# Windowed attention with two masked key blocks: merging the halves by a predicated copy, the sink as a score column, and a reordered unit loop

## The chip, the cores and the metric

The kernel runs on one core of one Trainium2 chip. The metric is the device time of one launch in microseconds. Engines are named as in the profile: PE is TensorE (matrix products and transposes), DVE is VectorE, ACT is ScalarE, POOL is GpSimd, SP is the queue that starts the DMAs.

## The reference, cut to what matters

Two layers of a decoder are computed for a prompt of 2048 tokens and for eight short sample sequences. The second layer's token mixer is sliding-window attention with 16 query heads, four key heads, head size 64, a bias that falls with distance, and one learned sink per head. For the prompt, 128 queries see the 128 keys of their own block and the 128 of the block before:

```python
qi = jnp.arange(BLOCK)[:, None]
si = jnp.arange(2 * BLOCK)[None, :]
dist = BLOCK + qi - si
valid = (dist >= 0) & (dist < WINDOW) & ((blk - 1) * BLOCK + si >= 0)
s = einsum(q, k) * HEAD_DIM ** -0.5 - slopes * dist
s = jnp.where(valid, s, NEG_INF)
p = softmax(concatenate([s, sink_col], axis=-1))[..., :-1]
o = einsum(p, v)
```

With BLOCK = WINDOW = 128, key j of the block before is valid for query i where j > i, and key j of the query's own block where j <= i. So of every pair of columns (j, 128 + j) exactly one is valid, except in the very first block, which has no block before it.

## The kernel before, in words

The tokens are worked through in five chunks of 4, 3, 3, 3 and 3 blocks of 128 prompt tokens; chunks 1 to 4 also carry two sample sequences of four tokens each. For each chunk the kernel runs a fixed list of projections (`ORDER`): the recurrent layer (X, G, O, Z, P), then the attention layer's keys, values, queries (k, v, q), its gate projections (g), and after the attention the output projections (o, z, p). A projection of one 128-wide output block is 24 matmuls (eight steps over the input features, three products each, since fp32 operands are split into a high and a low part). Every engine runs a program written out by hand in this order, and semaphores tie the engines together. DMAs have their own queue, SP, which only loads weights, tokens and states.

The change is in the attention stage, `attention(g)`, of which each engine has its own copy. It works in units: one unit is one block of 128 queries (`b`) and four heads (`quad`), so chunk 0 has 16 units and every other chunk 12. For a unit

- PE computes the scores of four heads against 256 keys (`unit_scores`, L1269, 12 matmuls into PSUM banks 4 and 5),
- DVE adds the distance bias and the mask (L1011, four operations of 256 columns; a masked place has the distance 1e33), takes the row maximum (L1000), compares it with the sink (L1001), negates it (L1002) and prepares the sink's exponent (L1003),
- ACT takes the exponentials with their row sums (L750, four operations) and that of the sink (L752),
- DVE adds the sink to the sums (L1024), inverts them (L1025) and multiplies the rows by the result (`divide`, L1027, four operations of 256 columns, each with a column of scalars),
- PE turns the probabilities (`unit_turn`, L1282, eight transposes of 128 by 128 into banks 6 and 7), ACT copies them to SBUF (L777), PE multiplies them by the values (`unit_values`, L1297), and ACT copies the result out (L782).

Between `unit_turn` and `unit_values` PE runs a slice of the gate projections g (`project`, L1213): four steps of eight per unit in chunks 1 to 4 (12 matmuls), three in chunk 0. About every second unit such a projection is complete, and DVE then halves and scales it (`half_gate`, L968), ACT takes its tanh (L717) and DVE makes the gate of it (`silu`, L978). POOL multiplies gate and attention output (L580, L585) and splits off the low part for the next projection (L591); in chunk 0 it also splits the incoming weights (L561) after ACT has made their high part (L680).

The order on PE inside a unit is: scores of unit u + 2, turn of u, projection slice, values of u. On DVE it is: scores work of u + 1, divide of u, then `silu` or `half_gate` if due.

## Time and profile before

| what | value |
|---|---|
| median of 3 runs | 2111.61 us (2110.57 to 2115.08) |
| the profiled execution | 2110.83 us, span 2109.0 us |
| PE busy | 1987.9 us, 94% of the span |
| DVE busy | 1203.0 us, 57% |
| ACT busy | 970.5 us, 46% |
| POOL busy | 627.1 us, 30% |
| chain that ended last, by engine | PE 67%, DVE 22%, ACT 5% |
| mean granted clock of PE | 0.972 of full speed |

The span is what the profiler covers of the execution; 1.8 us lie around it. Busy shares are averages over stages that differ: the projections outside the attention keep PE busy without a gap, so the attention stage has to be read by itself. The chain is followed back from the last instruction to what released it, so its shares tell which engine set the end, stage by stage.

### The profile page before, as it was taken

The numbers are of one execution on the slowest core, as the hardware profiler recorded it, in microseconds if no ns is written. First come the engines' busy times: TensorE is split into PE (matmuls) and PEld (weight loads), VectorE is DVE, ScalarE is ACT, GpSimd is POOL, SyncE is SP. The second block draws the span as 40 slices with busy tenths as digits, with TensorE's granted clock in tenths as the row PEclk, the third lists the DMA queues.
The fourth block names the chain that finished last, engine by engine and source line by source line (L and its number), as shares of the span: only waits on it lengthen the run. The fifth ranks groups of instructions, "written<-read, shape, count | busy, mean of one in ns | idle before, by whom it ended". The sixth has DMA issues, their size and how long they took to land.

```text
span 2109.0 us, 29173 instructions
## 1 busy us (share of the span) xinstructions
PE 1987.9 (94%) x11140; PEld 1788.6 (85%) x11140; DVE 1203.0 (57%) x2451; ACT 970.5 (46%) x1898; POOL 627.1 (30%) x545
## 2 busy tenths in 40 slices
PE   6889998899899999999999999999999999999997
PEld 4667886577789997998999789899987998999797
DVE  8874418845593338358442754774258459433944
ACT  5764435645463226346431544563236347322632
POOL 6465672366222112221211133121103212211221
PEclk9999998999999989999999899999999999999998
DMA  7567882277676752575867237677742676675255
GB/s 255 201 212 261 289 322 98 91 259 258 232 254 221 274 187 83 192 284 189 278 242 273 77 147 242 231 253 236 273 152 101 235 263 236 230 278 206 81 183 177
DMA packets 139466, 451.24 MB, mean 214 GB/s; under 512 B 41408, under 2 KB 83392, under 8 KB 95680
## 3 DMA queue, kind: packets, MB, share of 16 engines
q1 hardware_dynamic: 139328, 449.39, 60.3%
q8 instruction: 89, 1.46, 0.3%
q14 instruction: 49, 0.40, 0.1%
HBM read 362.82 MB, written 86.52 MB: 213 GB/s over the span
## 4 chain that ended last, share of the span: by engine, by line
PE 67%; DVE 22%; ACT 5%; issue 2%; POOL 2%; DMA 2%; SPq 0%; POOLq 0%; DVEq 0%; ACTq 0%
PE psum L1213 57%; DVE conv_out L928 3%; DVE scores L1027 3%; PE psum L1282 2%; PE psum L1297 2%; DVE lru_or_o L959 2%; DVE gate_tanh L978 2%; DVE scores L1011 2%; DVE row_max L1000 1%; PE psum L1245 1%; DVE conv_out L924 1%; DMA w_split<-w_cache 1%; DVE resid L995 1%; POOL w_split L561 1%; PE psum L1269 1%
## 5 line engine op out<-in xcount | busy, mean ns | idle before, releaser
L1213 PE MATMUL psum<-b_hi,w_split 128*128 128x392 f32 (+1 forms) x2880 | 814.9, 356 | 10.4 <-POOL b_lo L591 6.9
L1213 PE MATMUL psum<-a_hi,w_split 128*128 128x392 f32 (+1 forms) x2560 | 730.1, 360 | 8.9 <-DVE a_lo L897 4.2
L1213 PEld LDWEIGHTS psum<-b_hi,w_split 128*128 128x128 f32 x2880 | 536.4, 190 | 41.3 <-POOL b_lo L591 8.6
L1213 PEld LDWEIGHTS psum<-a_hi,w_split 128*128 128x128 f32 x2560 | 476.2, 190 | 44.2 <-issue 8.9
L1213 PE MATMUL psum<-b_lo,w_split 128*128 128x392 f32 (+1 forms) x1440 | 506.9, 352 | 0.0
L1213 PE MATMUL psum<-a_lo,w_split 128*128 128x392 f32 (+1 forms) x1280 | 450.1, 352 | 0.0
L1213 PEld LDWEIGHTS psum<-b_lo,w_split 128*128 128x128 f32 x1440 | 273.9, 190 | 11.6 <-issue 0.2
L570 POOL TENSOR_TENSOR square_sum<-square_sum,square 128x392 f32<-128x392 f32 (+1 forms) x140 | 154.2, 1101 | 434.3 <-ACT square L687 434.3
L1213 PEld LDWEIGHTS psum<-a_lo,w_split 128*128 128x128 f32 x1280 | 243.1, 190 | 19.6 <-issue 5.0
L580 POOL TENSOR_TENSOR gate_tanh<-gate_tanh,lru_or_o 128x384 f32<-128x384 f32 (+1 forms) x80 | 87.9, 1100 | 569.5 <-DVE gate_tanh L978 301.3
L561 POOL TENSOR_TENSOR w_split<-w_stage,w_split 128x1024 fp32r<-128x1024 f32 x68 | 166.1, 2444 | 148.1 <-ACT w_split L680 147.8
L687 ACT ACTIVATE square<-resid 128x392 f32<-128x392 f32 (+1 forms) x140 | 77.1, 551 | 269.2 <-DVE resid L1134 182.7
L1134 DVE TENSOR_TENSOR resid<-psum,resid 128x392 f32<-128x392 f32 (+1 forms) x80 | 47.3, 592 | 238.6 <-PE psum L1213 238.6
L968 DVE SCALAR_TENSOR_TENSOR gate_half<-psum,inv_rms 128x392 f32<-128x392 f32 (+1 forms) x120 | 70.6, 588 | 165.3 <-PE psum L1213 164.9
L750 ACT ACTIVATE scores<-scores,row_max_neg 128x256 f32<-128x256 f32 (+1 forms) x272 | 132.7, 491 | 50.9 <-DVE sink_exp L1003 26.4
L717 ACT ACTIVATE gate_tanh<-gate_half 128x392 f32<-128x392 f32 (+1 forms) x160 | 87.4, 546 | 125.6 <-DVE gate_half L968 125.0
L1175 DVE SCALAR_TENSOR_TENSOR q<-psum,inv_rms 128x392 f32<-128x392 f32 (+1 forms) x40 | 23.7, 592 | 165.5 <-PE psum L1213 165.5
L1282 PE MATMUL psum<-identity,scores 128*128 128x128 f32 x512 | 75.3, 294 | 40.3 <-DVE scores L1027 40.3
L928 DVE SCALAR_TENSOR_TENSOR conv_out<-conv_in,vec,conv_out 128x400 f32<-128x400 f32 (+1 forms) x120 | 104.0, 867 | 4.3
L1027 DVE TENSOR_SCALAR scores<-scores,row_sum 128x256 f32<-128x256 f32 (+1 forms) x272 | 104.2, 447 | 2.4
L1282 PEld LDWEIGHTS psum<-identity,scores 128*128 128x128 f32 x512 | 59.2, 148 | 54.2 <-DVE scores L1027 48.9
L1245 PE MATMUL psum<-conv_out,w_ri 128*128 128x400 f32 (+1 forms) x160 | 74.8, 595 | 31.1 <-DVE conv_out L928 31.1
(154 smaller groups left out, 2646.0 us busy)
## 6 DMA issues: line engine op xcount, KB each, us to landing
w_split<-w_cache SPq DMA_DIRECT2D x272, 1024.0 KB, 4.9
w_cache<-w_split SPq DMA_DIRECT2D x68, 1024.0 KB, 6.8
w_stage<-w_big SPq DMA_DIRECT2D x68, 512.0 KB, 5.6
w_split<-w_cache_small SPq DMA_DIRECT2D x64, 256.0 KB, 4.4
x_stage<-x SPq DMA_DIRECT2D x32, 192.0 KB, 4.9
resid<-x SPq DMA_DIRECT2D x4, 1536.0 KB, 8.9
y_out<-resid SPq DMA_DIRECT2D x3, 1536.0 KB, 10.1
w_cache_small<-w_split SPq DMA_DIRECT2D x16, 256.0 KB, 6.5
```

The source lines that it names most:

```text
L561: nc.gpsimd.tensor_tensor(W[:, j % RING, 1, 0:n, :], staged(j), W[:, j % RING, 0, 0:n, :].bitcast(F32), ALU.subtract).then_inc(w_lo.sem, 1)
L570: nc.gpsimd.tensor_tensor(acc, acc, square_of(g, o, k), ALU.add).then_inc(added[o].sem, 1)
L580: ins = nc.gpsimd.tensor_tensor(tg[:, 0:tp], tg[:, 0:tp], LR[:, t % 4, 0:tp], ALU.mult)
L687: nc.scalar.activation(acc if k == 0 else square_of(g, o, k), src, ACT.Square).then_inc(squared[o].sem, 1)
L717: nc.scalar.activation(TG[:, t % 3 if o else t % 2, 0:tt], GH[:, t % 2, 0:tt], ACT.Tanh).then_inc(tanh_done.sem, 1)
L750: nc.scalar.activation(sc[:, i, 0:width], sc[:, i, 0:width], ACT.Exp, bias=NM[:, s, i:i + 1], accum_out=DEN[:, s, i:i + 1])
L928: ins = v.scalar_tensor_tensor(xc, xb[:, k:k + fl], VEC[:, w:w + 1], xc, ALU.mult, ALU.add)
L968: v.scalar_tensor_tensor(GH[:, slot, 0:tt], bank(g, c), 0.5, r[:, 0:tt], ALU.mult, ALU.mult).then_inc(proj_free.sem, 1)
L1027: ins = v.tensor_scalar(sc[:, i, 0:width], sc[:, i, 0:width], DEN[:, s, i:i + 1], None, ALU.mult)
L1213: ins = nc.tensor.matmul(bank(g, c), W[:, s, w, k, :], x[:, k, 0:tt], start=(k == 0 and n == 0), stop=(k == nk - 1 and n == 2))
L1245: ins = nc.tensor.matmul(PSUM[:, 4 + 2 * (n % 2) + w, 0:fl], WRI[:, w * KT + n, :], XC[:, n % 2, 0:fl], start=True, stop=True)
L1282: ins = nc.tensor.transpose(PSUM[:, 6 + h, i * BLK:(i + 1) * BLK], SC[:, u % 3, i, h * BLK:(h + 1) * BLK], IDN[:])
```

## The change

For all blocks but the very first, DVE copies the scores of the valid older keys over the masked places of the newer half, in PSUM (`copy_predicated` with a constant mask `OLD`, 512 columns per unit, PSUM to PSUM). From there on a row has 128 columns instead of 256. The bias table's first slice is now the merged distance. The sink is written as column 128 of the scores (a four-column copy), so maximum and row sum take it in, and the operations L1001, L1002, L1003, L1024 of before and the sink's own exponential go away; the maximum comes out negated. The four multiplications by a column of scalars were there before; they are now 128 columns wide. PE turns four tiles instead of eight. With P the merged probabilities, the output is P times the newer values plus P, kept where the key is of the older block, times (older values minus newer values). So ACT copies 512 turned columns (`PT[:, 0]`), DVE writes the masked part beside them (`keep_old`, 512 columns, PSUM times an SBUF mask into `PT[:, 1]`), POOL makes the differences `VD` once per chunk, in the stage of the q projections, and PE runs as many value products as before, now against `V` and `VD`. The score products keep their 256 columns.

The order changes too. On PE the values of unit u - 1 now follow the turn of unit u, ahead of the projection slice; on DVE the divide of u comes first, then the scores work of u + 2, then `keep_old` of u. ACT copies the turned tile of u only after the values of u - 1 are done (`PT` has one buffer), and copies out unit u - 1 behind it. The turned tiles alternate between banks 6 and 7.

```diff
-            def row_max(s, sc, sink):
-                link(v.tensor_reduce(MX[:, s, :], sc, AX_X, ALU.max))
-                link(v.tensor_tensor(two(MX[:, s, :]), two(MX[:, s, :]), sink, ALU.max))
-                v.tensor_scalar(NM[:, s, :], MX[:, s, :], -1.0, None, ALU.mult)
-                v.tensor_tensor(two(ES[:, s, :]), sink, two(MX[:, s, :]), ALU.subtract).then_inc(nm_ready.sem, 1)
+            def row_max(s, sc, width):
+                v.tensor_reduce(NM[:, s, :], sc[:, :, 0:width + 1], AX_X, ALU.max,
+                                negate=True).then_inc(nm_ready.sem, 1)
...
+                v.tensor_copy(sc[:, :, BLK], VEC[:, V_SINK + 4 * quad:V_SINK + 4 * quad + 4])
+                if g or b:
+                    link(v.copy_predicated(new, OLD[:].bitcast(U32).unsqueeze(1).to_broadcast([128, 4, BLK]), old))
                 for i in range(4):
...
+                    ins = v.scalar_tensor_tensor(sc[:, i, 0:BLK], DIST[:, 0 if g or b else 2, :],
+                                                 -slope(head_at(2 * quad + i % 2, i // 2)), new[:, i, :],
                                                  ALU.mult, ALU.add)
...
+            def keep_old(g, u):
+                dve.wait_ge(pt_ready.sem, pt_ready.at(g, event(g, u) + 1))
+                v.tensor_tensor(PT[:, 1, :].rearrange("p (i q) -> p i q", i=4),
+                                PSUM[:, 6 + u % 2, :].rearrange("p (i q) -> p i q", i=4),
+                                OLD_T[:].unsqueeze(1).to_broadcast([128, 4, BLK]), ALU.mult).then_inc(pt_old.sem, 1)
...
                 for u in range(nu):
-                    if u + 1 < nu:
-                        unit_scores(g, u + 1)
...
+                    divide(g, event(g, u), 1 + u % 3, SC[:, u % 3], BLK)
+                    if u + 2 < nu:
+                        unit_scores(g, u + 2)
+                    keep_old(g, u)
...
-                for h in range(2):
-                    for i in range(4):
-                        ins = nc.tensor.transpose(PSUM[:, 6 + h, i * BLK:(i + 1) * BLK],
-                                                  SC[:, u % 3, i, h * BLK:(h + 1) * BLK], IDN[:])
+                for i in range(4):
+                    ins = nc.tensor.transpose(PSUM[:, 6 + u % 2, i * BLK:(i + 1) * BLK], SC[:, u % 3, i, 0:BLK], IDN[:])
...
+                pe.wait_ge(pt_old.sem, pt_old.at(g, u + 1))
...
+                    for h, vals in enumerate((V[:, b + 1], VD[:, b])):
...
                     unit_turn(g, u)
+                    if u:
+                        unit_values(g, u - 1)
...
-                    unit_values(g, u)
+                unit_values(g, nu - 1)
```

On DVE, one round of the unit loop in chunk 1 stood like this before (`row_sum` is the row sums, `sink_exp` the sink's exponent, `gate_half` a gate projection):

```order
L1024 TENSOR_TENSOR row_sum<-row_sum,sink_exp 128x4
L1025 RECIPROCAL row_sum<-row_sum 128x4
L1027 TENSOR_SCALAR scores<-scores,row_sum 128x256 x4
L1011 SCALAR_TENSOR_TENSOR scores<-dist,psum 128x256 x4
L1000 TENSOR_REDUCE row_max<-scores 128x4
L1001 TENSOR_TENSOR row_max<-row_max,vec 128x4
L1002 TENSOR_SCALAR row_max_neg<-row_max 128x4
L1003 TENSOR_TENSOR sink_exp<-vec,row_max 128x4
```

and the same round stands like this in the changed kernel (`vec` holds the sinks, `from_before` is the mask `OLD`, `probs_t` the turned probabilities):

```order
L1045 RECIPROCAL row_sum<-row_sum 128x4
L1047 TENSOR_SCALAR scores<-scores,row_sum 128x128 x4
L1031 COPY scores<-vec 128x4
L1033 COPY_PREDICATED psum<-from_before,psum 128x4x128
L1035 SCALAR_TENSOR_TENSOR scores<-dist,psum 128x128 x4
L1021 TENSOR_REDUCE row_max_neg<-scores 128x4
L1053 TENSOR_TENSOR probs_t<-psum,from_before_t 128x512
```

Four operations of four columns went, three operations came (L1031, L1033, L1053), and the wide ones are half as wide.

On PE, from the turn of one unit to the start of the next score products, it stood before (slice of chunk 1, `v` is the values):

```order
L1282 MATMUL psum<-identity,scores 128x128 x8
L1213 MATMUL psum<-b_hi,w_split 128x392
L1213 MATMUL psum<-b_lo,w_split 128x392
...
L1297 MATMUL psum<-probs_t,v 64x256 x4
L1269 MATMUL psum<-k_hi,a_hi 128x256
```

and now (`v_step` is `VD`):

```order
L1319 MATMUL psum<-identity,scores 128x128 x4
L1336 MATMUL psum<-probs_t,v 64x256
L1336 MATMUL psum<-probs_t,v_step 64x256
L1336 MATMUL psum<-probs_t,v 64x256
L1336 MATMUL psum<-probs_t,v_step 64x256
L1248 MATMUL psum<-b_hi,w_split 128x392
L1248 MATMUL psum<-b_lo,w_split 128x392
```

Four transposes of eight are gone, and the value products (those of the unit before) moved ahead of the projection slice.

## Rows read from the trace of the kernel before

**Rows 1.** Groups by line and form, whole span: busy us, mean ns, idle before it.
```profile
L1282 PE MATMUL psum<-identity,scores 128*128 128x128 f32 x512 | 75.3, 294 | 40.3 <-DVE scores L1027 40.3
```
**Rows 2.** Unit loops, chunks 0, 2, 3: us, busy PE, PEld, DVE, ACT, POOL, clock, DMA.
```profile
329.40:432.60 103.20, 85.07 (x557) 62.36 (x557) 91.01 (x215) 63.67 (x181) 31.59 (x19) 0.93 0.28 92
...
1176.00:1244.30 68.30, 62.56 (x445) 51.71 (x445) 55.27 (x159) 41.80 (x128) 14.60 (x18) 0.94 0.22 79
1564.80:1630.20 65.40, 59.63 (x445) 48.77 (x446) 55.31 (x159) 41.83 (x128) 14.60 (x18) 0.99 0.23 82
```
**Rows 3.** Timeline of PE, one unit of chunk 2: start us, us, instructions.
```profile
1183.27 1.10 PE L1282 MATMUL psum<-identity,scores 128*128 128x128 f32 x8
1184.12 0.42 PE L1213 MATMUL psum<-b_hi,w_split 128*128 128x392 f32 x1
1184.38 0.34 PE L1213 MATMUL psum<-b_lo,w_split 128*128 128x392 f32 x1
...
1186.42 1.09 PE L1297 MATMUL psum<-probs_t,v 128*64 128x256 f32 x8
...
1188.36 1.09 PE L1282 MATMUL psum<-identity,scores 128*128 128x128 f32 x8
```
**Rows 4.** Timeline of DVE, one unit of chunk 2 without a hold.
```profile
1206.91 1.41 DVE L1011 SCALAR_TENSOR_TENSOR scores<-dist,psum 128x256 f32<-128x256 f32 x4
...
1208.35 1.22 DVE L1000 TENSOR_REDUCE row_max<-scores 128x4 f32<-128x1024 f32 x1
...
1209.60 0.16 DVE L1001 TENSOR_TENSOR row_max<-row_max,vec 128x4 f32<-128x4 f32 x1
...
1210.14 0.18 DVE L1025 RECIPROCAL row_sum<-row_sum 128x4 f32<-128x4 f32 x1
1210.35 1.14 DVE L1027 TENSOR_SCALAR scores<-scores,row_sum 128x256 f32<-128x256 f32 x4
...
1211.41 0.56 DVE L968 SCALAR_TENSOR_TENSOR gate_half<-psum,inv_rms 128x392 f32<-128x392 f32 x1
...
1211.88 0.41 DVE L1011 SCALAR_TENSOR_TENSOR scores<-dist,psum 128x256 f32<-128x256 f32 x1
```
**Rows 5.** Groups by line and form, whole span: operations near in shape to new ones.
```profile
L1134 DVE TENSOR_TENSOR resid<-psum,resid 128x512 f32<-128x512 f32 x16 | 11.1, 692 | 56.8 <-PE psum L1213 56.8
L1000 DVE TENSOR_REDUCE row_max<-scores 128x4 f32<-128x528 f32 x4 | 2.8, 703 | 0.1
L766 ACT ACTIVATE probs_t<-psum 128x512 f32<-128x512 f32 x4 | 2.4, 598 | 10.8 <-PE psum L1318 10.8
L652 POOL TENSOR_TENSOR a_lo<-q,a_hi 128x384 fp32r<-128x384 f32 x32 | 32.5, 1014 | 133.3 <-ACT a_hi L858 133.3
```
**Rows 6.** Timeline of DVE, chunk 2: the samples' divide, 132 columns wide, and what follows.
```profile
1161.34 0.88 DVE L1027 TENSOR_SCALAR scores<-scores,row_sum 128x132 f32<-128x132 f32 x4
1162.14 1.40 DVE L1011 SCALAR_TENSOR_TENSOR scores<-dist,psum 128x256 f32<-128x256 f32 x4
```
**Rows 7.** Timeline, chunk 0: a POOL operation and a divide that meet.
```profile
345.82 2.36 POOL L561 TENSOR_TENSOR w_split<-w_stage,w_split 128x1024 fp32r<-128x1024 f32 x1 [9.96 <-ACT w_split L680]
...
345.92 3.20 DVE L1027 TENSOR_SCALAR scores<-scores,row_sum 128x256 f32<-128x256 f32 x4
```
**Rows 8.** Single lines, whole span: ns min/median/max.
```profile
L1011 DVE SCALAR_TENSOR_TENSOR scores<-dist,psum x256: 404/414/424, 320.9 to 2002.8; 128x256 f32<-128x256 f32 x128
...
L917 DVE COPY conv_in<-conv_carry x40: 155/162/1301, 31.9 to 1780.5; 128x3 f32<-128x3 f32 x40
```
**Rows 9.** The divide's groups by form in the loops of chunk 2 and chunk 0.
```profile
L1027 DVE TENSOR_SCALAR scores<-scores,row_sum 128x256 f32<-128x256 f32 x44 | 14.8, 401 | 0.4
...
L1027 DVE TENSOR_SCALAR scores<-scores,row_sum 128x256 f32<-128x256 f32 x60 | 35.6, 656 | 0.5
```
**Rows 10.** Timeline of PE, chunk 1: a stall and the matmuls behind it.
```profile
845.22 1.09 PE L1282 MATMUL psum<-identity,scores 128*128 128x128 f32 x8 [2.23 <-DVE scores L1027]
...
846.44 0.53 PE L1213 MATMUL psum<-b_lo,w_split 128*128 128x392 f32 x1
```

More of the change, by code:

```diff
@@ L245, in build @@
         TI = sb("gate_i", [FLAT])
-        SC = sb_at("scores", [3, 4, 2 * BLK], F32, t_at)
-        PT = sb_at("probs_t", [2, 4 * BLK], F32, t_at + 12288)
+        SC = sb_at("scores", [3, 4, SW + 1], F32, t_at)
+        PT = sb_at("probs_t", [2, 4 * BLK], F32, t_at + 6400)
+        VD = sb_at("v_step", [max(CHUNK_BLOCKS), NKV * HD], F32, t_at + 10496)
+        assert 12 * 4 * (SW + 1) <= 6400 and 10496 + 4 * max(CHUNK_BLOCKS) * NKV * HD <= 16384
         VT = sb_at("v_t", [2, T0], F32, t_at)
@@ L260, in build @@
         DIST = sb("dist", [3, BLK])
+        OLD = sb("from_before", [BLK])
+        OLD_T = sb("from_before_t", [BLK])
         TBS = sb("bias_s", [2, CSEQ * SW])
@@ L391, in build @@
         pt_ready = stage("pt_ready", events)
+        pt_old = stage("pt_old", units)
+        v_step = stage("v_step", 1)
         o_done = stage("o_done", events)
@@ L647, in _ @@
                                                 ALU.subtract).then_inc(k_lo.sem, 1)
+                    if kind == "q" and m == 4:
+                        nb = blocks_of(g)
+                        if g:
+                            pool.wait_ge(carry_done.sem, carry_done.at(g - 1, 1))
+                        pool.wait_ge(v_ready.sem, v_ready.at(g, 2))
+                        nc.gpsimd.tensor_tensor(VD[:, 0:nb, :], V[:, 0:nb, :], V[:, 1:nb + 1, :],
+                                                ALU.subtract).then_inc(v_step.sem, 1)
                     if kind == "q":
@@ L1018, in unit_scores @@
                 dve.wait_ge(s_read.sem, s_read.at(g, ev + 1))
-                row_max(1 + u % 3, sc, two(VEC[:, V_SINK + 4 * quad:V_SINK + 4 * quad + 4]))
+                row_max(1 + u % 3, sc, BLK)
             def divide(g, ev, s, sc, width):
                 dve.wait_ge(exp_done.sem, exp_done.at(g, ev + 1))
-                link(v.tensor_tensor(DEN[:, s, :], DEN[:, s, :], ES[:, s, :], ALU.add))
                 link(v.reciprocal(DEN[:, s, :], DEN[:, s, :]))
@@ L1033, in attention @@
                     dve.wait_ge(k_out.sem, 16)
[L1034 to L1035 removed]
+                s4 = SC[:, 2]
                 if seqs_of(g):
                     dve.wait_ge(s_done.sem, s_done.at(g, 1))
[L1038 to L1039 removed]
+                    v.tensor_copy(s4[:, :, SW].rearrange("p (a s) -> p a s", a=2),
+                                  two(VEC[:, V_SINKS:V_SINKS + 2 * SG])[:, :, 0:CSEQ])
+                    v.tensor_tensor(s4[:, :, 0:SW].rearrange("p (a s) w -> p a s w", a=2),
+                                    PSUM[:, 4:6, 0:CSEQ * SW].rearrange("p a (s w) -> p a s w", w=SW),
+                                    TBS[:].rearrange("p a (s w) -> p a s w", w=SW), ALU.add).then_inc(s_read.sem, 1)
                     dve.wait_ge(s_read.sem, s_read.at(g, 1))
[L1041 removed]
+                    row_max(0, s4, SW)
                 half_gate(g, G1, 0, R)
@@ L1183, in _ @@
                             ins.then_inc(q_ready.sem, 1)
+                    if c == Q1 and g == 0:
+                        v.tensor_scalar(OLD[:], DIST[:, 1, :], BLK, None, ALU.is_lt)
+                        v.tensor_tensor(DIST[:, 0, :], DIST[:, 1, :], DIST[:, 2, :], ALU.min)
+                        link(v.tensor_scalar(OLD_T[:], DIST[:, 2, :], BLK, None, ALU.is_lt))
+                        link(v.scalar_tensor_tensor(OLD_T[:], DIST[:, 2, :], 0.0, OLD_T[:], ALU.is_gt, ALU.mult))
                     if c == G1 - 1:
```

80 lines of the change are left out of this document (40 added, 40 removed).

## The prediction

> **What bounds the kernel now.** Start with the profile's first part and the chain: TensorE is busy nearly all the time and holds most of the chain, so outside the attention only its own work counts, and the change touches none of that work. Then look for the place where TensorE waits. The list of groups shows it: the transposes of the probabilities (L1282) had 40.3 us of idle time ahead of them, all of it waiting for VectorE's divide [rows 1]. So the five attention loops are to be read by themselves [rows 2]: the loop of chunk 0 lasts 103.2 us, of which TensorE is busy 85.1 and VectorE 91.0; that of chunk 3 lasts 65.4 us, with 59.6 and 55.3. (Chunk 1 is like chunk 2, at 68.3 us, and chunk 4 like chunk 3.)
>
> Two timelines give the pace of one unit. TensorE, not held, comes from turn to turn in 1188.36 - 1183.27 = 5.09 us, and eight transposes take 1184.12 - 1183.27 = 0.85 us of that [rows 3]. VectorE, not held, takes 1211.88 - 1206.91 = 4.97 us: score operations 1.44, maximum 1.25, the small operations to the divide 0.75, divide 1.06, one gate operation 0.47 [rows 4]. So the two are almost level, and in 12 units their own lines (61 and 60 us) leave little of the 65.4. What tips it is the third engine: a divide that meets a GpSimd operation of 2.36 us takes 3.20 us instead of 1.14 [rows 4, 7]. In the loop of chunk 2 the divides' mean is 401 ns where an unheld one takes 285 (1.14 / 4): 44 of them lose 5.1 us. In chunk 0 it is 656 ns, and 60 lose 22.3 us [rows 4, 9].
>
> **The change, part by part.** TensorE: 256 of 512 transposes go [rows 1], four per unit, 0.85 / 2 = 0.43 us; its unit falls to 4.66 us. Value products and score products stay as they are. In a loop of 12 units that is 5.1 us, over all 64 units 27.2 us. This is the gain if TensorE sets the pace.
>
> VectorE, per unit. A column costs (1220 - 703) / (1024 - 528) = 1.04 ns in the maximum [rows 4, 5].
> - The score operations lose 512 columns: 1.44 - 0.53 = 0.91. The maximum goes from 1024 to 516 columns: 1.25 - 0.53 = 0.72.
> - Of the small operations only the reciprocal stays: 0.21 (1210.14 to 1210.35).
> - The divide: four of 132 columns take 1162.14 - 1161.34 = 0.80 [rows 6], against 1.06.
> - New: the sink's copy, 0.16 by the median of a three-column copy, of which about half lies beside its neighbour: 0.1 [rows 8].
> - New: the predicated copy, 512 columns. No row shows this operation. Its lower end is 0.53 (512 columns at 1.04 ns, no fixed part), its upper end 1.22, if it reads both places and so walks 1024 columns like the maximum. I take 0.72, the add of 512 columns from PSUM (0.69) [rows 5] and 0.03 for the wait behind it, since it too reads one PSUM and one SBUF operand per column. A gain is excluded: the operation is new.
> - New: `keep_old`, the same form, 0.69, of which some 0.05 overlap: 0.65.
>
> The sum is 0.91 + 0.72 + 0.21 + 0.80 + 0.1 + 0.72 + 0.65 = 4.11 against 4.50, so with a gate operation 4.58 against 4.97. VectorE's line too falls by only 0.39 us per unit, 4.7 in 12 units. The narrowing is nearly eaten by the three new operations.
>
> [...] The row with 0.80 has a duration for nearly this width, so it is used.
>
> What takes the rest back:
> - Holds. The divides stay, so the 5.1 us (chunk 0: 22.3) stay. The sink's copy is a new operation of the kind that is held: such a copy takes 155 ns at best and 1301 at worst, while the score operations, which read PSUM and one SBUF operand, never exceed 424 [rows 8]. GpSimd is busy 14.6 of 65.4 us, 22% [rows 2], so about two or three of 12 copies meet it and wait half of a 1.0 us operation [rows 5]: 1.3 us per loop. In chunk 0 it is busy 31% of the time, with operations up to 2.36 us [rows 2, 7]: five copies at about 0.8, 4 us.
> - A new ring. `keep_old` waits for ScalarE's copy (0.60 [rows 5]), that for the values of the unit before (1.09 [rows 3]), these for the turn (0.43), and that for the divide: 2.1 us plus four hand-overs of some 0.05 make 2.3. VectorE meanwhile does copy, predicated copy, scores and maximum, 0.1 + 0.72 + 0.91 + 0.72 = 2.45. That covers the ring only if TensorE is free when the divide ends; if it is still in its projection slice or score products, VectorE waits inside `keep_old`, and behind it the gate operation and the next divide wait, which release TensorE. I put 0.18 per unit, 2.1 us per loop, as an estimate from the 0.15 us of slack. The ring also replaces slack that is used up now: TensorE already idles 65.4 - 59.6 = 5.8 us per loop though its own line is shorter.
>
> Per loop of chunks 1 to 4: -4.7 + 1.3 + 2.1 = -1.3. Chunk 0, 16 units: -6.2 + 4 + 2.9 = 0.7, with TensorE's -6.8 as its other bound; I take -2, nearer the VectorE sum, since VectorE is busy 91 of 103 us there. Together 4 x -1.3 - 2 = **-7 us**.
>
> Costed at nothing: GpSimd's value differences (768 or 1024 columns, some 2 us at 1014 ns for 384, once per chunk), since it stands idle 133.3 us in the q stages waiting for ScalarE [rows 5]; without that cover the five would cost 10 us. The masks made once in chunk 0, and the shorter exponentials and PSUM copies on ScalarE, which is busy 42 of 65.4 us [rows 2], count nothing either. The division "in four products by a column of scalars" was there before, so nothing is won by that but the width. No DMA moves.
>
> From the profiled execution's own 2110.83 us, which is 0.8 below the median, -7 gives **2104 us**. A measurement of this kernel can tell some 0.2%, 4 us, from no change.
>
> **The rivals.**
> - TensorE sets the pace (0.12). The holds fall where VectorE has slack, and the loops go to its line: chunk 3 from 59.6 - 5.1 = 54.5 plus some 2.5 of idle to 57, so 8.4 less; four times that, and 11 in chunk 0: 45 us less, 2066. For it: values a unit later give the turn more room. Against: VectorE's line is as long as TensorE's and is the one that is held.
> - Slower: the predicated copy costs its upper end (0.18). At 1.22 each unit gains 0.53 us on VectorE, in some 51 units inside the loops 27 us: 2131, or some 2125 where TensorE's waits absorb part. It decides from about 0.72 + 7 / 51 = 0.86 us per copy on. For it: one operation reads and writes the same PSUM banks. Against: the adds from PSUM show nothing of the kind.
> - Slower: stalls lower TensorE's clock (0.12). Behind a wait of 2.23 us the matmuls run at 0.53 instead of 0.34 each, the lower of the clock's two levels [rows 3, 10]; a slice of 12 then loses about 1.5 us. If the held copies and the ring make two more such waits per loop, that is 15 us: 2119.
> - The clock rises (0.08). Chunk 2's loop ran at a mean granted clock of 0.94 and took 68.3 us, chunk 3's at 0.99 and 65.4 [rows 2]; if fewer transposes let chunks 1 and 2 run like chunk 3, 5.8 us more go: 2098. [...]
> - The work is hidden either way and nothing moves (0.05): 2111.
>
> **How the numbers follow.** The forecast has 0.45, with a range of its own from 2094 to 2112 (ring and held copies at nothing, or at double); of this 0.30 is faster by over 0.2% and 0.15 within. With 0.12 and 0.08 from the faster rivals, faster has 0.50. Within has 0.15, 0.05 and 0.04 from the low ends of the slower ones, 0.24; slower 0.26. The range leaves out most of the first rival and the top of the second: 2080 to 2128.
>
> **What would show it.** Right: L1319 (the turn) with half the instructions of L1282 and still 30 to 50 us of idle ahead of it, released by L1047; loops of 63 to 65 us in chunks 3 and 4; VectorE busy some 50 us in them, with waits ahead of `keep_old` for ScalarE's copy; copies L1031 with a maximum over 1 us; L1033 near 0.69 us. Wrong: loops of 58 us with hardly any idle time on TensorE (first rival), L1033 over 0.86 us (second), or a granted clock under 0.94 in the loops (third).

## The result, and the profile after

The changed kernel takes 2089.6 us (median of 4 runs, 2087.94 to 2094.5) against 2113.1 for the kernel before in the same measurement: a ratio of 0.9893 [0.9872, 0.9914], 23.5 us or 1.1% faster. The forecast was 2104 in a range from 2080 to 2128: the time lies in the range and has the forecast sign, but the gain is more than three times the 7 us that the sum gave.

The page's first part of the changed kernel gives the engines' busy time:

```profile
PE 1964.2 (94%) x10884; PEld 1754.7 (84%) x10884; DVE 1171.4 (56%) x2370; ACT 912.7 (44%) x1830; POOL 636.1 (30%) x550
```

TensorE does 23.7 us less work (1987.9 before), VectorE 31.6 us less (1203.0). The span falls by 21.7 us, from 2109.0 to 2087.3. So the time fell by about what TensorE was relieved of.

A loop is taken in this document from the start of its first turn to the end of its last value products. The loops of chunks 0 to 4 of the changed kernel answer to [rows 2] (us, busy PE, PEld, DVE, ACT, POOL, granted clock, DMA share, GB/s):

```profile
329.64:422.25 92.61, 78.64 (x493) 53.38 (x493) 78.81 (x199) 49.42 (x166) 31.98 (x19) 0.95 0.29 102
772.84:838.47 65.63, 58.43 (x399) 44.86 (x397) 54.58 (x150) 31.69 (x117) 14.04 (x18) 0.96 0.23 81
1159.47:1223.28 63.81, 56.44 (x399) 43.64 (x397) 54.55 (x150) 31.69 (x117) 14.02 (x18) 0.99 0.23 84
1545.56:1611.18 65.62, 59.39 (x399) 46.24 (x397) 54.59 (x150) 31.68 (x117) 14.05 (x18) 0.94 0.23 82
1930.52:1994.51 63.99, 56.61 (x399) 43.81 (x397) 54.56 (x150) 31.68 (x117) 14.02 (x18) 0.99 0.24 84
```

The sums over the five loops, the kernel before first, then the changed one:

```profile
sum 370.61, PE 329.59 PEld 263.43 DVE 312.03 ACT 230.75 POOL 90.03; mean PE 65.92 PEld 52.69 DVE 62.41 ACT 46.15 POOL 18.00
sum 351.66, PE 309.51 PEld 231.93 DVE 297.08 ACT 176.16 POOL 88.11; mean PE 61.90 PEld 46.39 DVE 59.42 ACT 35.23 POOL 17.62
```

The loops fell by 19.0 us; the other 2.7 of the span's 21.7 lie outside them and are not accounted for, and the rest of the 23.5 is the distance of the two profiled executions from the medians. Chunk 0's loop fell from 103.2 to 92.6 us, by 10.6, where the forecast had -2; the other four fell from 267.4 to 259.1 together, by 8.4, where it had 4 x -1.3 = -5.2. Two of them have to be read together: chunk 2's loop went from 68.3 to 63.8 us while its granted clock rose from 0.94 to 0.99, and chunk 3's from 65.4 to 65.6 while its clock fell from 0.99 to 0.94. TensorE's idle time in the five loops (length less busy time) did not fall: 41.0 us before, 42.2 now.

The groups by line and form of the changed kernel give the prices (busy us, mean ns, idle before):

```profile
L1319 PE MATMUL psum<-identity,scores 128*128 128x128 f32 x256 | 44.7, 300 | 42.3 <-DVE scores L1047 42.0
```

```profile
L1047 DVE TENSOR_SCALAR scores<-scores,row_sum 128x128 f32<-128x128 f32 x256 | 92.5, 423 | 2.2
L1035 DVE SCALAR_TENSOR_TENSOR scores<-dist,psum 128x128 f32<-128x128 f32 x256 | 56.4, 282 | 2.1
L1021 DVE TENSOR_REDUCE row_max_neg<-scores 128x4 f32<-128x516 f32 x64 | 44.2, 691 | 2.2
L1053 DVE TENSOR_TENSOR probs_t<-psum,from_before_t 128x512 f32<-128x512 f32 x64 | 44.0, 688 | 33.8 <-ACT probs_t L799 33.6
L1033 DVE COPY_PREDICATED psum<-from_before,psum 128x512 f32<-128x512 uint32 x60 | 41.2, 686 | 0.0
L1031 DVE COPY scores<-vec 128x4 f32<-128x4 f32 x64 | 11.1, 173 | 19.1 <-PE psum L1304 19.1
```

The prices are as forecast: 686 ns for the predicated copy (0.69 plus a wait of 0.03 was taken), 688 for `keep_old`, 691 for the maximum. TensorE's wait for the divide has not moved, 42.0 us against 40.3 [rows 1]. VectorE has a new wait of 33.6 us ahead of `keep_old`, for ScalarE's copy, and the sink's copies are hardly ever held (mean 173 ns, the longest 611).

To compare kernels I use two measures. One is the time from the start of one unit's turn to that of the next, a step, from TensorE's timelines; a unit that meets no GpSimd operation is called undisturbed. The other is the length of the loops. Both are read from the execution that was profiled; its time stands beside the median, and the two differ by up to 6 us:

| kernel | median, us | profiled, us | undisturbed unit, us | loop of chunk 0 | loops of chunks 1 to 4 together |
|---|---|---|---|---|---|
| before | 2113 | 2110.8 | 5.09 | 103.2 | 267.4 |
| changed | 2089.6 | 2089.1 | 4.85 | 92.6 | 259.1 |
| e1 turns twice | 2113.5 | 2119.1 | 5.28 | 97.6 | 283.4 |
| e3 before, values behind the turn | 2112.1 | 2112.1 | 5.28 | 101.6 | 271.3 |
| e4 values at the slice's end | 2074.2 | 2078.2 | 5.16 | 93.3 | 242.5 |
| e8 e4 and `keep_old` earlier | 2053.9 | 2054.0 | 4.65 | 87.3 | 232.4 |
| e13 before, GpSimd out of the way | 2072.1 | 2073.3 | 5.09 | 84.3 | 251.1 |
| e14 changed, GpSimd out of the way | 2049.0 | 2049.4 | 4.85 | 77.9 | 231.7 |

### The profile page after: what moved, and what is told of

It reads as the page before. It is cut to its first block, busy times and chain, and to the rows that moved or that the text cites. A ratio compares the mean times of both kernels' runs of the same rounds, so it can differ in the third digit from the quotient of the medians.

```text
span 2087.3 us, 28585 instructions
## 1 busy us (share of the span) xinstructions
PE 1964.2 (94%) x10884; PEld 1754.7 (84%) x10884; DVE 1171.4 (56%) x2370; ACT 912.7 (44%) x1830; POOL 636.1 (30%) x550
## 3 DMA queue, kind: packets, MB, share of 16 engines
q8 instruction: 87, 1.43, 0.3%
## 4 chain that ended last, share of the span: by engine, by line
PE 64%; DVE 24%; ACT 5%; issue 3%; POOL 2%; DMA 2%; SPq 0%; POOLq 0%; DVEq 0%; ACTq 0%
PE psum L1248 54%; DVE conv_out L949 4%; DVE scores L1047 3%; PE psum L1336 3%; DVE lru_or_o L980 2%; DVE gate_tanh L999 2%; PE psum L1319 2%; PE psum L1304 1%; DMA w_split<-w_cache 1%; DVE probs_t L1053 1%; DVE conv_out L945 1%; DVE resid L1016 1%; DVE gate_half L989 1%; DVE gate_i L975 1%; PE psum L1280 1%
## 5 line engine op out<-in xcount | busy, mean ns | idle before, releaser
L1248 PE MATMUL psum<-b_hi,w_split 128*128 128x392 f32 (+1 forms) x2880 | 814.7, 356 | 13.6 <-POOL b_lo L596 9.2
L566 POOL TENSOR_TENSOR w_split<-w_stage,w_split 128x1024 fp32r<-128x1024 f32 x68 | 168.4, 2477 | 120.4 <-ACT w_split L693 120.4
L763 ACT ACTIVATE scores<-scores,row_max_neg 128x129 f32<-128x129 f32 (+1 forms) x272 | 106.0, 395 | 55.0 <-PE psum L1371 28.1
L1205 DVE SCALAR_TENSOR_TENSOR q<-psum,inv_rms 128x392 f32<-128x392 f32 (+1 forms) x40 | 23.7, 592 | 164.7 <-PE psum L1248 164.7
L1280 PE MATMUL psum<-conv_out,w_ri 128*128 128x400 f32 (+1 forms) x160 | 72.9, 582 | 31.6 <-DVE conv_out L949 31.6
L1248 PE MATMUL psum<-p_hi,w_split 128*128 128x392 f32 (+1 forms) x320 | 101.5, 358 | 0.0
L1047 DVE TENSOR_SCALAR scores<-scores,row_sum 128x128 f32<-128x128 f32 (+1 forms) x272 | 96.0, 415 | 2.4
L799 ACT ACTIVATE probs_t<-psum 128x512 f32<-128x512 f32 x64 | 38.4, 600 | 134.1 <-PE psum L1336 129.7
```

What stands on the lines that cost most here:

```text
L566: nc.gpsimd.tensor_tensor(W[:, j % RING, 1, 0:n, :], staged(j), W[:, j % RING, 0, 0:n, :].bitcast(F32), ALU.subtract).then_inc(w_lo.sem, 1)
L763: ins = nc.scalar.activation(sc[:, i, 0:width + 1], sc[:, i, 0:width + 1], ACT.Exp, bias=NM[:, s, i:i + 1], accum_out=DEN[:, s, i:i + 1])
L1047: ins = v.tensor_scalar(sc[:, i, 0:width], sc[:, i, 0:width], DEN[:, s, i:i + 1], None, ALU.mult)
L1248: ins = nc.tensor.matmul(bank(g, c), W[:, s, w, k, :], x[:, k, 0:tt], start=(k == 0 and n == 0), stop=(k == nk - 1 and n == 2))
L1280: ins = nc.tensor.matmul(PSUM[:, 4 + 2 * (n % 2) + w, 0:fl], WRI[:, w * KT + n, :], XC[:, n % 2, 0:fl], start=True, stop=True)
```

## The experiments

Three theories stood at the start: V, VectorE's shorter line made the gain, above all with shorter holds in chunk 0; T, TensorE's shorter work made it; O, the new order of the value products made it. From e5 on two more are used: R, a closed way round through several engines sets the pace of a unit; H, holds by GpSimd lie on that way.

### Is it TensorE, VectorE or the order? (e1 to e4)

**e1**, the change with the old number of transposes:

```diff
-                for i in range(4):
+                for i in (0, 1, 2, 3, 0, 1, 2, 3):
                     ins = nc.tensor.transpose(PSUM[:, 6 + u % 2, i * BLK:(i + 1) * BLK], SC[:, u % 3, i, 0:BLK], IDN[:])
```

> The changed kernel with every unit's four transposes issued twice, the first time into the same place, so TensorE issues as many transposes as before the change. Theory V (the gain is VectorE's shorter line, chunk 0's shorter holds above all): the 27 us of transposes fall into the 42.0 us that TensorE waits for the turn, and the time rises by at most 10 us, to 2090 to 2100 us. Theory T (the gain is TensorE's own shorter work): nearly all of the gain goes, 2107 to 2117 us. Theory O (the gain is the order: the values of a unit after the turn of the next): as V, under 10 us.

Measured: 2113.48 us, a ratio to before of 1.0013 [1.0002, 1.0024]. The whole gain is gone; V and O fall in this form. The 42 us in which TensorE waits for the turn took nothing up:

```profile
L1319 PE MATMUL psum<-identity,scores 128*128 128x128 f32 x512 | 74.5, 292 | 43.2 <-DVE scores L1047 43.2
```

The wait is still 43.2 us beside 29.8 us more of transposes. It isn't slack. Two turns in a row in chunk 2 show it, first in the changed kernel, then in e1 (PE's timelines):

```profile
1173.72 0.66 PE L1319 MATMUL psum<-identity,scores 128*128 128x128 f32 x4 [0.21 <-DVE scores L1047]
1179.73 0.66 PE L1319 MATMUL psum<-identity,scores 128*128 128x128 f32 x4 [1.09 <-DVE scores L1047]
...
1187.32 1.09 PE L1319 MATMUL psum<-identity,scores 128*128 128x128 f32 x8 [0.20 <-DVE scores L1047]
1193.76 1.09 PE L1319 MATMUL psum<-identity,scores 128*128 128x128 f32 x8 [1.09 <-DVE scores L1047]
```

The step grows from 6.01 to 6.44 us, by 0.43, and the wait of 1.09 stays: by the program's order the divide that ends it stands behind `keep_old` of the unit before, which waits by way of ScalarE's copy for that unit's turn, so longer transposes push the divide back too. In undisturbed units, where nothing waits, the step grows by the same 0.43 (4.85 to 5.28).

**e2**, the predicated copy twice:

```diff
                 if g or b:
                     link(v.copy_predicated(new, ...))
+                    link(v.copy_predicated(new, ...))
```

> The changed kernel with the predicated copy issued twice in a row, 60 further copies of 0.69 us on VectorE, 41 us in all. Theory V: VectorE sets the pace, and 20 to 41 us come on: 2110 to 2131 us. Theory T: VectorE waits 33.6 us in front of keep_old and 19.1 us in front of the sink's copy, and these take it: under 10 us, 2090 to 2100 us. Theory O: in between.

Measured: 2103.75 us, 0.9967 [0.9954, 0.9979]. Of 41 us of VectorE work, 14 arrive in the time. VectorE is near the line but does not set it in the changed kernel: the undisturbed unit goes from 4.85 to 5.11 us, by 0.26 of the 0.69, so VectorE had 0.43 us to spare there.

**e3**, the order alone, on the kernel before:

```diff
                     unit_turn(g, u)
+                    if u:
+                        unit_values(g, u - 1)
...
-                    unit_values(g, u)
+                unit_values(g, nu - 1)
```

(ScalarE's copy of the probabilities then waits for `o_done` of unit u - 1, and its copy of the output stands a unit later.)

> The kernel before with only the order of the change: TensorE's value products of unit u-1 stand behind the turn of unit u, and ScalarE's copy of the probabilities waits for them. Theory O: this alone brings half of the gain or more, 2090 to 2102 us. Theories V and T: within 5 us of the kernel before, 2106 to 2118 us.

Measured: 2112.14 us, 1.000 [0.9991, 1.001]. The order brings nothing by itself, but its undisturbed unit is 5.28 us, 0.19 longer than 5.09: value products right behind the turn cost TensorE 0.19 us that they don't cost at the end of a slice (TensorE has no wait in these steps). That nothing moves is a sum of opposite parts: the order also decides which divides meet a GpSimd operation. The divide's groups in the loops of chunk 0 and chunk 2 of e3:

```profile
L1036 DVE TENSOR_SCALAR scores<-scores,row_sum 128x256 f32<-128x256 f32 x60 | 31.5, 587 | 0.5
...
L1036 DVE TENSOR_SCALAR scores<-scores,row_sum 128x256 f32<-128x256 f32 x44 | 20.2, 521 | 0.4
```

Before, they were 35.6 and 14.8 [rows 9]. Unheld sets of four take 1.14 us, so 15 are 17.1 and 11 are 12.5: by the order alone the divides of chunk 0's loop lose 14.4 us in place of 18.5, and those of each other loop 7.7 in place of 2.3.

**e4**, the reverse on the changed kernel:

```diff
                     unit_turn(g, u)
-                    if u:
-                        unit_values(g, u - 1)
...
-                unit_values(g, nu - 1)
+                    unit_values(g, u)
```

> The changed kernel with the value products of unit u at the end of its projection slice, where they stood before the change. Theory O: half of the gain or more goes, 2100 to 2115 us. Theories V and T: within 6 us of the changed kernel, 2084 to 2096 us.

Measured: 2074.18 us, 0.9824 [0.9806, 0.9842]: 15 us faster than the changed kernel, which no theory had. The new order is the worse one here, and the holds move back again. The divide's groups in the loops of chunk 0 and chunk 2, first in the changed kernel, then in e4:

```profile
L1047 DVE TENSOR_SCALAR scores<-scores,row_sum 128x128 f32<-128x128 f32 x60 | 26.8, 508 | 0.5
...
L1047 DVE TENSOR_SCALAR scores<-scores,row_sum 128x128 f32<-128x128 f32 x44 | 15.3, 410 | 0.4
...
L1047 DVE TENSOR_SCALAR scores<-scores,row_sum 128x128 f32<-128x128 f32 x60 | 29.7, 557 | 0.5
...
L1047 DVE TENSOR_SCALAR scores<-scores,row_sum 128x128 f32<-128x128 f32 x44 | 12.7, 350 | 0.4
```

Here unheld sets take 0.88 us (e14), 13.2 for 15 and 9.7 for 11. So the divides of the changed kernel lose 13.6 us in chunk 0 and 5.6 in each other loop, those of e4 16.5 and 3.0. Two timelines of e4, DVE and PE, show the pace of a unit:

```profile
1553.69 0.68 DVE L1053 TENSOR_TENSOR probs_t<-psum,from_before_t 128x512 f32<-128x512 f32 x1
1554.47 0.66 PE L1336 MATMUL psum<-probs_t,v 128*64 128x256 f32 x4 [0.43 <-issue]
1558.85 0.68 DVE L1053 TENSOR_TENSOR probs_t<-psum,from_before_t 128x512 f32<-128x512 f32 x1
1559.64 0.66 PE L1336 MATMUL psum<-probs_t,v 128*64 128x256 f32 x4 [0.44 <-issue]
```

`keep_old` ends at 1554.37 and the values start 0.1 us later, after 0.43 us of idle time on TensorE. (The view puts it down to "issue", but `unit_values` waits for `pt_old`, which `keep_old` raises.) The pace of 5.16 us is a ring of values, score products, VectorE's work on them up to `keep_old`, values. Yet the 44 steps of chunks 1 to 4 take 227.3 us, and 44 times 5.16 is 227.0: in this order a divide that is held a little costs next to nothing (a set of 1.43 us in place of 0.88 stands in a step of 5.21), since the turn stands beside that ring with room to spare. The longest holds still cost: in chunk 0 a set of 5.03 us stands in a step of 8.06. In the changed order the divide is itself in a ring, divide, turn, values of the unit before, ScalarE's copy, `keep_old`, divide, so a hold goes straight into the pace.

### Where a transpose costs, and where `keep_old` belongs (e7, e8, e11, e12)

**e7** is e4 with the edit of e1.

> The kernel of e4 (the changed one, the values of unit u at the end of its projection slice) with the four transposes issued twice. In that kernel a unit's period of 5.16 us is the ring values, score products, VectorE's work up to keep_old, values; the turn stands beside it. Theory R (the transposes cost what they do because they lie in the ring turn, values of the unit before, PSUM copy, keep_old): at most 10 us over e4, 2070 to 2085. Theory T (every transpose costs TensorE time wherever it stands): 20 to 27 us over e4, 2094 to 2101.

Measured: 2075.01 us, 0.9824 [0.981, 0.9838], against 2074.18 for e4. The same 256 transposes that cost 24 us in e1 cost nothing measurable: they fill TensorE's 0.43 us of waiting. T in its plain form falls.

**e8** moves `keep_old` ahead of the row maximum, **e11** does the same without the order of e4:

```diff
                 ins.then_inc(s_read.sem, 1)
+                if between is not None:
+                    keep_old(g, between)
                 dve.wait_ge(s_read.sem, s_read.at(g, ev + 1))
                 row_max(1 + u % 3, sc, BLK)
```

(`unit_scores(g, u + 2, u)` hands it the unit.)

> The kernel of e4 with keep_old moved ahead of the row maximum of the unit whose scores are being made. Theory R: VectorE's part of that ring gets 0.69 us shorter, TensorE's wait of 0.43 us ahead of the values goes in most units, and some 15 to 25 us come off: 2050 to 2060. Theory T: nothing changes for TensorE's work, within 5 us of e4, 2069 to 2080.

Measured: 2053.85 us, 0.9727 [0.9711, 0.9744], 20 us under e4. The undisturbed unit is 4.65 us: TensorE's own line is reached (4.66 in the prediction).

> The changed kernel with keep_old ahead of the row maximum, and the values behind the turn as they are there. The ring (divide, turn, values of the unit before, PSUM copy, keep_old) is not shortened, and the maximum of 0.69 us no longer lies inside VectorE's wait for it but behind it. Theory R, the ring is level with TensorE's line: a unit's period goes from 4.85 to some 5.4 us, 15 to 35 us slower, 2105 to 2125. Theory T, TensorE's line alone sets the pace: within 6 us, 2084 to 2096.

Measured: 2107.05 us, 0.9967 [0.9954, 0.998], 17 us slower than the changed kernel by the same edit that made e4 20 us faster. The waits of e11 show why:

```profile
L1055 DVE TENSOR_TENSOR probs_t<-psum,from_before_t 128x512 f32<-128x512 f32 x64 | 44.3, 692 | 71.2 <-ACT probs_t L799 71.2
```

VectorE waits 71.2 us in `keep_old` (33.6 in the changed kernel), with the maximum and the next divide queued behind it; the shortest common step is 5.23 us in place of 4.85. The ring of the prediction exists. In e11 the maximum (0.69 us) lies on it; without it, an estimate of 5.23 - 0.69 = 4.54 us is left for the changed kernel's ring, just below TensorE's line of 4.85.

**e12** is e8 with the edit of e1.

> The kernel of e8 with the four transposes issued twice. In it nothing but TensorE's own line is left to set an undisturbed unit (4.65 us). Theory T: 0.43 us for nearly each of 64 units, 18 to 27 us over e8, 2072 to 2081, where in e4 the same transposes cost 1 us. Theory R: under 10 us over e8, 2054 to 2064.

Measured: 2080.82 us, 0.9846 [0.983, 0.9862], 27.0 us over e8. The three runs together: transposes cost their full time where TensorE's line is the longest way round a unit (changed kernel: 24 us, e8: 27), and 1 us where TensorE waits 0.43 us a unit for another ring (e4).

### Holds by GpSimd (e5, e6, e10, e13, e14)

**e5** and **e6** put one operation in the place of a unit's four divides, in the changed kernel and in the one before:

```diff
-                for i in range(4):
-                    ins = v.tensor_scalar(sc[:, i, 0:width], sc[:, i, 0:width], DEN[:, s, i:i + 1], None, ALU.mult)
-                ins.then_inc(p_ready.sem, 1)
+                v.tensor_tensor(sc[:, :, 0:width], sc[:, :, 0:width],
+                                DEN[:, s, :].unsqueeze(2).to_broadcast([128, 4, width]), ALU.mult).then_inc(p_ready.sem, 1)
```

> The changed kernel with the four divides of a unit as one product of two tensors, 512 columns with the column of reciprocals repeated along them. At 1.04 ns a column it takes some 0.6 us, against 0.88 for four that meet no GpSimd operation. Theory H (the holds lie on the ring divide, turn, values of the unit before, PSUM copy, keep_old, divide): if the new form is not held, the divides fall from 96.0 us to about 41, and the time by 15 to 35 us, to 2055 to 2075. Theory T (only TensorE's own work counts): within 5 us of the changed kernel, 2085 to 2095. If the new form is held as the old one is, maximum durations over 1.5 us stay in its rows.

Measured: 2073.35 us, 0.981 [0.9795, 0.9825], 16 us under the changed kernel. The new form takes 0.69 us unheld in place of 0.88, but it is held too: the longest, 2.65 us, ran beside a GpSimd operation (L566) of 2.52. Its line in e5 (ns min/median/max):

```profile
L1046 DVE TENSOR_TENSOR scores<-scores,row_sum x68: 691/693/2652, 327.0 to 1968.7; 128x512 f32<-128x512 f32 x64, 128x528 f32<-128x528 f32 x4
```

> The kernel before with the four divides as one product of two tensors of 1024 columns, some 1.1 us, as long as four that are not held. Theory H: without holds the loops go to TensorE's line, 10 to 30 us less: 2083 to 2103. Theory T: within 5 us of the kernel before, 2107 to 2118.

Measured: 2090.88 us, 0.9893 [0.9878, 0.9908], as fast as the whole change, with an operation that is no shorter when nothing meets it (its median is 1224 ns, four took 1.14 us [rows 4]). Groups by form of e6, PE and DVE:

```profile
L1281 PE MATMUL psum<-identity,scores 128*128 128x128 f32 x512 | 74.9, 293 | 26.4 <-DVE scores L1026 25.8
```

```profile
L1026 DVE TENSOR_TENSOR scores<-scores,row_sum 128x1024 f32<-128x1024 f32 x64 | 84.7, 1324 | 2.2
```

64 unheld operations would be 78.3 us, so 6.4 are lost; the four short ones lost 28 (104.2 us of busy time in all, against 64 times 1.14 and the samples' 3.2). TensorE's wait falls from 40.3 to 25.8 us, and the time by 22, about the 21.6 us that the divides lose less: before the change a hold came through nearly one to one.

**e10** leaves the sink's copy out in all but three units of a chunk.

```diff
-                v.tensor_copy(sc[:, :, BLK], VEC[:, V_SINK + 4 * quad:V_SINK + 4 * quad + 4])
+                if u < 3:
+                    v.tensor_copy(sc[:, :, BLK], VEC[:, V_SINK + 4 * quad:V_SINK + 4 * quad + 4])
```

> The changed kernel with the sink's copy made for the first three units of a chunk alone; the other units' softmax finds an old value in the sink's column. The prediction put 1.3 us per loop and 4 us in chunk 0 on copies that are held, 9.2 us in all: if that term stands, 2078 to 2083. If the copies hardly meet a GpSimd operation (their mean is 173 ns), within 4 us of the changed kernel, 2085 to 2094.

Measured: 2089.51 us, 0.9886 [0.9871, 0.9901], against 2089.6. The term of 9.2 us for held sink copies is nothing.

**e13** and **e14** cut GpSimd's operations of the loops to 8 columns, in the kernel before and in the changed one. The other columns are left unmade, and the output projection takes the high part twice, so TensorE's work is the same:

```diff
-                        split_low(g, c + AHEAD)
+                        split_low(g, c + AHEAD, 8)
...
+                tp = 8 if o == "y1" else tp
                 ins = nc.gpsimd.tensor_tensor(tg[:, 0:tp], tg[:, 0:tp], LR[:, t % 4, 0:tp], ALU.mult)
...
-                tt = tokens_of(g)
+                tt = 8 if o == "y1" else tokens_of(g)
...
-                        a, b, o = (Bhi, Blo, "y0") if kind == "O" else (Ahi, Alo, "y1")
+                        a, b, o = (Bhi, Blo, "y0") if kind == "O" else (Ahi, Ahi, "y1")
```

> The kernel before with GpSimd's operations of the attention loops cut to 8 columns: gate times attention output, its low part, and in chunk 0 the low part of the weights; the output projection takes the high part in the low part's place, so TensorE's work is the same, and those values are left unmade. If the time above TensorE's line (about 49 us over the five loops) is held divides, 30 to 45 us go: 2068 to 2083. If it is waiting of another kind, under 15 us: 2098 to 2113.

> The changed kernel with the same operations cut. If the time above its line (about 40 us) is held divides, 22 to 37 us go: 2052 to 2067, and it is then 10 to 20 us under the other run of this pair, the lines' difference of 0.24 us in 59 units. If holds do not explain the 7.7 us that chunk 0 gave beyond the line, the pair still differs by 20 us or more.

Measured: 2072.09 us, 0.9809 [0.9795, 0.9823], and 2048.98 us, 0.9697 [0.9683, 0.9711]. GpSimd's operations cost the kernel before 40 us and the changed one 41. No divide is held any more: the longest single operation takes 357 ns in e13 and 291 in e14, against 2471 and 2460 with GpSimd at work. The loop of chunk 0 and the sum of the five, e13 first, then e14:

```profile
328.25:412.51 84.26, 81.42 (x557) 59.33 (x557) 70.73 (x215) 62.92 (x181) 4.11 (x19) 0.97 0.33 113
sum 335.32, PE 322.19 PEld 256.42 DVE 276.76 ACT 228.66 POOL 20.96; mean PE 64.44 PEld 51.28 DVE 55.35 ACT 45.73 POOL 4.19
...
328.67:406.56 77.89, 76.75 (x493) 52.77 (x493) 62.79 (x199) 49.27 (x166) 4.47 (x19) 0.96 0.37 123
sum 309.54, PE 302.47 PEld 228.45 DVE 252.90 ACT 175.72 POOL 20.11; mean PE 60.49 PEld 45.69 DVE 50.58 ACT 35.14 POOL 4.02
```

So GpSimd cost the loops 35.3 us before the change (370.6 to 335.3) and 42.1 after it (351.7 to 309.5). The divides alone lost 18.5 + 4 x 2.3 = 27.7 us and 13.6 + 4 x 5.6 = 36.0, so it is mostly held divides in both; the gate operation is held too (L978 is busy 60.1 us over the whole span before and L981, the same operation, 49.6 in e13), and how much of the rest lies with TensorE's clock (chunk 0's loop had 0.93 before and has 0.97 in e13) was not taken apart. But the pair still differs by 23.1 us, so the change's gain as a whole is not a gain in holds. TensorE's timeline of e14, four turns of chunk 2 in a row, shows the line bare, each 4.85 us after the last and none with idle time ahead:

```profile
1157.32 0.66 PE L1322 MATMUL psum<-identity,scores 128*128 128x128 f32 x4
1162.16 0.66 PE L1322 MATMUL psum<-identity,scores 128*128 128x128 f32 x4
1167.01 0.66 PE L1322 MATMUL psum<-identity,scores 128*128 128x128 f32 x4
1171.86 0.66 PE L1322 MATMUL psum<-identity,scores 128*128 128x128 f32 x4
```

In e13 the steps are not all at the line: turns in chunk 2 at 1158.61 and 1164.26, and at 1184.99 and 1191.00, lie 5.65 and 6.01 us apart (PE's timeline):

```profile
1158.61 1.09 PE L1285 MATMUL psum<-identity,scores 128*128 128x128 f32 x8
1164.26 1.09 PE L1285 MATMUL psum<-identity,scores 128*128 128x128 f32 x8 [0.48 <-DVE scores L1030]
...
1184.99 1.09 PE L1285 MATMUL psum<-identity,scores 128*128 128x128 f32 x8
1191.00 1.09 PE L1285 MATMUL psum<-identity,scores 128*128 128x128 f32 x8
```

In the first step TensorE waits 0.48 us for the divide ahead of the turn; in the second the values wait 0.65 us for ScalarE's copy of the probabilities:

```profile
1188.87 1.09 PE L1300 MATMUL psum<-probs_t,v 128*64 128x256 f32 x8 [0.65 <-ACT probs_t L780]
```

### The parts put together (e9)

**e9** is e8 with the single divide of e5.

> The kernel of e8 with the single divide of e5. The holds that are left in e8's divides (85.1 us against some 59 if none were held) fall, as they did from the changed kernel to e5: 5 to 14 us under e8, 2040 to 2049. If e8 is already set by TensorE's line everywhere, within 4 us of it, 2050 to 2058.

Measured: 2045.54 us, 0.9681 [0.9667, 0.9695]: 44 us under the changed kernel and 68 under the one before, the fastest kernel of this study. TensorE still waits 17.2 us for the divide, and the single divides are held as in e5:

```profile
L1048 DVE TENSOR_TENSOR scores<-scores,row_sum 128x512 f32<-128x512 f32 x64 | 65.5, 1023 | 2.2
```

## Why the prediction was right in sign and wrong in size

The five loops fell from 370.6 to 351.7 us, by 19.0. Without GpSimd's operations they go from 335.3 (e13) to 309.5 (e14), by 25.8; that is taken here as the worth of the shorter work (with the new place of the values in it), and the difference as what the holds take back or give. By the prediction's terms:

| term | forecast, us | measured, us |
|---|---|---|
| chunks 1 to 4: shorter work | 4 x -4.7 = -18.8 | 251.1 to 231.7 = -19.4 |
| chunks 1 to 4: taken back by held copies and the ring | 4 x 3.4 = +13.6 | -8.4 + 19.4 = +11.0 |
| chunk 0: shorter work | -6.2 | 84.3 to 77.9 = -6.4 |
| chunk 0: taken back by held copies and the ring | 4 + 2.9 = +6.9; with -6.8 as the other bound, -2 was taken in all | -10.6 + 6.4 = -4.2 |

- **The step that failed** is the sum for chunk 0: "-6.2 + 4 + 2.9 = 0.7 ... I take -2". The loop gave 10.6, more than even the other bound of 6.8. The shorter work was worth 6.4, as forecast, but nothing was taken back, and 4.2 us came on top. The sink's copies cost nothing (e10), and the ring adds nothing to a unit that no hold meets (e14's units are at TensorE's line while VectorE waits 27.4 us in `keep_old`). The premise "The divides stay, so the 5.1 us (chunk 0: 22.3) stay" was wrong twice. Its figures set the mean of one operation against a quarter of a set, 285 ns, but an unheld operation takes 349 by the median and overlaps the next one; by busy time the divides of chunk 0 lost 18.5 us and those of chunk 2 lost 2.3. And the losses did not stay: chunk 0's fell to 13.6 us, by 4.9, and those of the other loops rose to 5.6 each, by 13.2 together, in line with the -4.2 and +11.0 of the table. The new order did this for the most part, and the prediction had no term for it: the order alone moves the losses of the kernel before from 18.5 and 2.3 to 14.4 and 7.7 (e3), and taking it out of the changed kernel moves them from 13.6 and 5.6 to 16.5 and 3.0 (e4).
- **Which engine sets the pace.** The sum went by VectorE's line (-0.39 us per unit), and named TensorE's as a rival. The pace of undisturbed units is TensorE's: 5.09 to 4.85, which is -0.43 for four transposes and +0.19 for the new place of the values (e3). Over 64 units that is 15 us of the 25.8. TensorE's idle time gives another 6 (13.1 us in e13's loops, 7.1 in e14's, length less busy time): steps that lay above the line, with TensorE waiting for VectorE or ScalarE as in e13's two steps, and no longer do. The last 4 are not assigned. That the estimate by VectorE's line came so near (-25.0 forecast for the five loops, -25.8 measured) is in part luck.
- **What takes the rest back in chunks 1 to 4** had about the right size, 13.6 against 11.0, and the wrong form. Sink copies are hardly held, and the ring costs nothing by itself; it is the divides, which lose 3.3 us more per loop, and the ring passes their holds on. The meeting itself looks like this: after ScalarE's copy of an output (L775) GpSimd starts, and the gate operation (L999, 0.56 us unheld in e14) and the divide behind it (0.88) stretch. The timeline of the changed kernel in chunk 3:

```profile
1563.50 0.38 ACT L775 ACTIVATE lru_or_o<-psum 128x256 f32<-128x256 f32 x1
1564.02 1.02 POOL L585 TENSOR_TENSOR gate_tanh<-gate_tanh,lru_or_o 128x384 f32<-128x384 f32 x1 [39.99 <-ACT lru_or_o L775]
1564.24 1.22 DVE L999 SCALAR_TENSOR_TENSOR gate_tanh<-gate_tanh,gate_half 128x392 f32<-128x392 f32 x1
...
1565.49 1.00 POOL L585 TENSOR_TENSOR gate_tanh<-gate_tanh,lru_or_o 128x384 f32<-128x384 f32 x1
1565.58 1.58 DVE L1047 TENSOR_SCALAR scores<-scores,row_sum 128x128 f32<-128x128 f32 x4
```

- **Right:** the prices of the new operations, the wait ahead of the transposes (30 to 50 us of idle ahead of L1319, released by L1047), VectorE's wait ahead of `keep_old`, the loops of chunks 3 and 4 (65.6 and 64.0 us against 63 to 65), GpSimd's value differences at nothing (the time outside the loops did not rise), and that most of what is saved in chunks 1 to 4 is taken back. Two signs failed: no sink copy took over 1 us, and VectorE's busy time in these loops is 54.6 us, not the forecast 50, since the divides there are held more.
- **The rivals.** "TensorE sets the pace" was right in mechanism and gave 45 us, too much: it had neither the 0.19 us nor the holds, since it let TensorE's idle time fall to 2.5 us per loop. The predicated copy did not cost its upper end (686 ns). The two clock rivals explain little. Stalls did not lower the clock on the whole: the mean granted clock went from 0.972 to 0.976. (The two levels that the prediction speaks of are a granted clock of 0.50, from 847 to 849 us of the kernel before, behind the wait of 2.23 us [rows 10], and of 1.00, from 1184 to 1186 us.) That fewer transposes raise it was a supposition of the prediction and is not borne out either: over all its runs e1, with the old number of transposes, has a median of 0.977, the changed kernel 0.974, and the kernel before in e1's measurement 0.970, while e1 and the kernel before take the same time. In chunk 0 the clock went from 0.93 to 0.95; by the missing share of the two loops (7.2 and 4.6 us) that is worth at most 2.6 of the 10.6 us, an estimate. e10, whose kernel differs by sink copies alone, had 0.93 there and took 93.2 us in place of 92.6:

```profile
326.88:420.10 93.22, 80.32 (x493) 54.31 (x493) 77.33 (x186) 49.27 (x166) 31.96 (x19) 0.93 0.30 101
```

- **The divide's price.** The prediction took it from the row of nearly the same width: four of 132 columns last 0.88 us, 0.80 to the start of the next operation [rows 6]. Four of 128 columns that nothing holds last 0.88 us too (e14), and the shortest single one of the changed kernel 271 ns: the row was right.

## What to carry to other kernels

Before costing an edit by an engine's length, write down for one unit the closed ways round (which engine waits for which, back to the start) and price each: here the same 256 transposes were worth 24 and 27 us where they lay on the longest one (e1, e12), and 1 us where they did not (e7), in three orders of one program. Waiting time seen on the pacing engine is no slack for new work if what ends it waits for that engine's earlier work in turn: in e1 the wait was still 43.2 us beside 29.8 us more of transposes. A new order also changes which operations meet another engine's, so holds read from the old trace cannot be carried over: the order alone moved the lost time of chunk 0's divides by 4.1 us one way and that of each other loop by 5.4 the other. The divides, which GpSimd's operations hold, were better kept out of the longest ring (e4, 15 us under the changed kernel) or issued once and not in four pieces (e5, 16 us under it) than only made narrower: in the changed kernel, half as wide and in the new order, they lost 36.0 us in the loops, 27.7 before.

## What the runs showed of the hardware

- One multiplication of 1024 columns lost 6.4 us over 64 units to GpSimd's operations (e6) where four of 256 columns lost 28 (the kernel before). A product of two SBUF tensors is held like the product with a column of scalars (691 ns at best, 2652 at worst in e5; 271 and 2460 in the changed kernel). With GpSimd's operations cut to 8 columns no product with a column of scalars took over 357 ns (e13), against 2471 before.
- Halving the width of a divide saved only a quarter of its time: four of 256 columns take 1.14 us [rows 4], four of 128 take 0.88 (e14), and one of 512 takes 0.69 (e5).
- A predicated copy of 512 columns within PSUM, with its mask in SBUF, takes 686 ns, as `keep_old`, a product of that width, does (688); both are means of the changed kernel.
- The place of the value products is worth 0.19 us of TensorE's time per unit: right behind the transposes it is 5.28 (e3) against 5.09, and 4.85 against 4.65 (e8). Why was not tried.
